# Paged decode in a hybrid decoder step on Trainium2: the order of weighing chunks, the last page gather, the score maxima and the latent division

## The chip, the cores and the metric

The kernel runs on one core of one Trainium2 chip. The metric is the device time of one execution in microseconds (us), as the median of several runs. A profile comes from one further execution that a hardware profiler records.

## The reference

One decoder layer is computed for two groups of requests that share the weights: a prompt of 512 tokens with 16 meta tokens ahead of it, and 8 decode samples of one token, each with a paged past of 4096 positions. The layer has a combined input projection, multi-head latent attention, a retention branch, a gated merge, two layer norms and a convolutional FFN. What the change touches is the latent attention of the 8 samples:

```python
def mla_sample(q_nope, q_rope, c_new, kr_new, c_past, kr_past, w_uk, w_uv):
    ...
    q_abs = jnp.einsum('bthn,chn->bthc', q_nope, w_uk)
    s_past = jnp.einsum('bthc,bsc->bhts', q_abs, c_past) + jnp.einsum('bthr,bsr->bhts', q_rope, kr_past)
    s_new = jnp.einsum('bthc,buc->bhtu', q_abs, c_new) + jnp.einsum('bthr,bur->bhtu', q_rope, kr_new)
    ...
    s = jnp.concatenate([s_past.astype(jnp.float32), s_new], -1) * scale
    p = jax.nn.softmax(s, axis=-1).astype(c_new.dtype)
    o_lat = jnp.einsum('bhts,bsc->bthc', p[..., :past], c_past) + jnp.einsum('bhtu,buc->bthc', p[..., past:], c_new)
```

`c_past` and `kr_past` are the cached latent rows (256 wide) and rotary rows (32 wide) of 32 pages of 128 positions, found by `page_table`.

## The kernel before, in words

The program is written engine by engine; each engine's list is in the order of its code, and semaphores are the only ties. The prompt's projections, retention and attention come first, then the eight samples, then merge, norms and FFN. The change is in the sample stage alone.

**Pages.** GpSimd (POOL) gathers a sample's pages by indirect DMA: four gathers of latent rows (`chunk_pair`, line 656; chunks 0-1, 2-3, 4-5 and 6-7 of 8) and one of rotary rows (`rope_page`, line 663), in the order 0-1, 2-3, rope, 4-5, 6-7. There are three sets of latent page buffers, so a gather for sample b waits until the same pair of chunks of sample b-3 has been weighed (`pv_chunk`) and until all earlier chunks have been turned (`page_turned`). POOL runs these in order: what waits holds all gathers behind it.

**Vector engine (DVE).** `sample_dve(b)` (line 1668) transposes ("turns") the chunks of sample b+1 (`turn_chunk`, L1546) and its rotary rows (`turn_rope`, L1638), and handles the softmax maxima of sample b: `scores_back` (L1644, L1646) takes the maxima over positions, `max_rows` (L1651, L1653) reduces them over partitions after TensorE has transposed them. It also divides the weighted latent of sample b-1 by its sum (`latent_out`, L1663) and inverts the sum of sample b (`inv_sum`, L1659). Eight chunks go through one set of turned tiles in two halves.

**TensorE (PE).** `sample(b)` (line 2590) scores sample b against its turned pages in two halves (`score_half`, L2525: 32 matmuls on latent rows and 4 on rotary rows, each recorded twice), transposes the partial scores (`turn_parts`, L2535), scores the new token (`score_new`, L2542, L2544), transposes the maxima (`max_turn`, L2552) and spreads them (`max_spread`, L2556). Of sample b-1 it sums the exponentials (`sum_spread`, L2561) and weighs the eight chunks (`weigh_chunk`, L2582, and L2587 for the new token). Of sample b-2 it turns the weighted latent (`latent_turn`, L2569).

**ScalarE (ACT).** After `max_spread` it copies the maxima (L1000) and takes the exponentials (L1004), and it copies partial scores (L1012) and weighted latents (L1018) out of PSUM.

The order around the change on PE, for samples 1 to 6, is: first matmul row of the first score half, `max_spread` of the sample before, rest of the first half, `latent_turn`, `sum_spread`, chunks 0 and 1, parts, chunk 2, second half, chunk 3, parts, new token, chunks 4 and 5, `max_turn`, chunks 6 and 7. In the last sample all chunks from 2 on come ahead of the second half.

Of the kernel before, what the change touches and what calls it, by code (L numbers as in the profile page):

```python
# [46 lines left out]
NCH = 8  # L47
# [113 lines left out]
def build(nc, ins, outs):  # L161
    ctx = ExitStack()
    with ctx:
# [211 lines left out]
        S = sems  # L375
# [272 lines left out]
        @block.gpsimd  # L648
        def _(pool):
            chain = Count(S["pool_own_order"])  # L650
            turned = Count(S["ln_turned"])
            
            pair_rows = ins["cache_kv_latent"][0].rearrange("n (q r) c -> (n q) (r c)", q=16)
            rope_rows = ins["cache_k_rope"][0].rearrange("n (q r) c -> (n q) (r c)", q=4)

            def chunk_pair(b, c):

                nc.gpsimd.indirect_dma_start(  # L658
                    out=page_pair(b, c).rearrange("p r c -> p (r c)"), out_offset=None,
                    in_=pair_rows, in_offset=bass.IndirectOffsetOnAxis(ap=IDX2[:, b, c // 2:c // 2 + 1], axis=0)  # L660
                ).then_inc(page_sem(b, c), 16)

            def rope_page(b):
                nc.gpsimd.indirect_dma_start(
                    out=PGR[:, b % 2, :, :].rearrange("p r c -> p (r c)"), out_offset=None, in_=rope_rows,
                    in_offset=bass.IndirectOffsetOnAxis(ap=IDX[:, b, NCH:NCH + 1], axis=0)
                ).then_inc(S[f"rope_pages{b % 2}"], 16)

            pool.wait_ge(S["idx_ready"], 1)
            pool.wait_ge(S["uk_T_ready"], 4)  # L670
            for c in range(0, NCH, 2):
                if c:
                    pool.wait_ge(S["probs_ready"], 6 * NT + c)
                chunk_pair(0, c)
            attn_done = Count(S["attn_done"], start=1)
            pool.wait_ge(attn_done.sem, attn_done.after(4))
            pool.wait_ge(S["out_stored"], 16 * 7)
            rope_page(0)
            for b in range(1, DEC):
                for c in range(0, NCH, 2):  # L680
                    if b >= 3:
                        pool.wait_ge(S["pv_chunk"], (b - 3) * NCH + c + 2)
                    pool.sem_inc(S["go_on"])
                    turned = (b - 1) * NCH + c
                    if turned > 0:
                        pool.wait_ge(S["page_turned"], turned)
                    chunk_pair(b, c)
                    if c == 2:
                        if b >= 2:
                            pool.wait_ge(S["rope_turned"], b - 1)  # L690
                        rope_page(b)
# [554 lines left out]
        def _(dve):  # L1246
# [6 lines left out]
            def lo(n, nk=8):  # L1253

                at_, ks = place(n, nk)
                dve.wait_ge(whi.sem, whi.after())
                V.tensor_tensor(WL[:, at_, ks], RAW[:, at_, ks], WH[:, at_, ks].bitcast(F32), ALU.subtract  # L1257
                                ).then_inc(s_wsplit, 1)
# [381 lines left out]
            def scores_back(par, b):  # L1640

                dve.wait_ge(s_full.sem, s_full.after())
                new = PS[0:DEC, 6, 256:264]
                V.tensor_scalar(new, new, SMALL[0:DEC, b + 16:b + 17], None, ALU.add).then_inc(S["s_bank_free"], 1)  # L1644
                dve.wait_ge(bank_free.sem, bank_free.after())
                V.reduce_max(SSM[:, par, 0:8], PS[:, 6, 0:264].rearrange("p (k h) -> p h k", h=HEADS), AX  # L1646
                             ).then_inc(S["mx_ready"], 1)

            def max_rows(par):
                dve.wait_ge(mxt.sem, mxt.after())  # L1650
                V.reduce_max(SSM[0:8, par, 8:9], PS[0:8, 7, 0:P], AX).then_inc(chain.sem, 1)  # L1651
                dve.wait_ge(chain.sem, chain.after())
                V.tensor_scalar(SSM[0:8, par, 16:24], IDENT[0:8, 0:8], SSM[0:8, par, 8:9], None, ALU.mult  # L1653
                                ).then_inc(S["dg_ready"], 1)
# [13 lines left out]
            def sample_dve(b):  # L1668

                par, more = b % 2, b + 1 < DEC  # L1670
                if more:
                    for c in range(4):
                        turn_chunk(b + 1, c)
                scores_back(par, b)
                if more:
                    turn_rope(b + 1)
                max_rows(par)
                if more:
                    turn_chunk(b + 1, 4)
                    turn_chunk(b + 1, 5)  # L1680
                else:
                    dve.wait_ge(S["ab_hi"], 1)
                    V.tensor_tensor(BL[:], BT[:, :, DEAD:], BH[:].bitcast(F32), ALU.subtract).then_inc(S["ab_split"], 1)
                    lo(N_MERGE + 1, 4)
                if more:
                    turn_chunk(b + 1, 6)
                    turn_chunk(b + 1, 7)
                if b:
                    latent_out(1 - par, b - 1)
                inv_sum(par)  # L1690

            attn_done = Count(S["attn_done"], start=1)
# [389 lines left out]
        def _(pe):  # L2082
# [464 lines left out]
            def max_turn(par):  # L2547

                if mx.n:
                    pe.wait_ge(rs.sem, rs.after())  # L2550
                pe.wait_ge(mx.sem, mx.after())
                T.transpose(PS[0:8, 7, 0:P], SSM[:, par, 0:8], IDENT).then_inc(S["mx_turned"], 1)  # L2552
# [37 lines left out]
            def sample(b):  # L2590

                par, prev, last = b % 2, b > 0, b == DEC - 1
                pe.wait_ge(q_staged.sem, q_staged.after())
                score_half(b, 0, range(1))
                if prev:
                    max_spread(1 - par)
                score_half(b, 0, range(1, 9))
                if b >= 2:  # L2600
                    latent_turn(b - 2)
                if prev:
                    sum_spread(1 - par)
                    weigh_chunk(b - 1, 0)
                    weigh_chunk(b - 1, 1)
                turn_parts(0)
                if prev:
                    for c in range(2, NCH if last else 3):
                        weigh_chunk(b - 1, c)
                score_half(b, 1)  # L2610
                if prev and not last:
                    weigh_chunk(b - 1, 3)
                turn_parts(1)
                score_new(b)
                if prev and not last:
                    for c in range(4, NCH):
                        if c == 6:
                            max_turn(par)
                        weigh_chunk(b - 1, c)
                elif not last:  # L2620
                    max_turn(par)

            q_staged, parts = Count(S["q_staged"]), Count(S["parts_back"])
            pe.wait_ge(S["rows_set"], 1)
# [317 lines left out]
```

## Time and profile before

| | us |
|---|---|
| median of 3 runs | 1009.57 (1007.57 to 1011.45) |
| the profiled execution, own time | 1018.73 |
| its span in the trace | 1016.8 |
| from the first score half of sample 0 (403.5) to the last one of sample 7 (509.9) | 106.4 |

Over the span PE is busy for 96%, DVE for 66%, ACT for 39%. A timeline row gives start, duration, engine, line, operation and tiles, number of instructions, and, in brackets, the idle time of the engine just ahead with what ended it. PE's ends are modelled, its starts are recorded. Times are us from the span's start.

### The profile page before, as it was taken

The numbers are of one execution on the slowest core, as the hardware profiler recorded it, in microseconds if no ns is written. First come the engines' busy times: TensorE is split into PE (matmuls) and PEld (weight loads), VectorE is DVE, ScalarE is ACT, GpSimd is POOL, SyncE is SP. The second block draws the span as 40 slices with busy tenths as digits, with TensorE's granted clock in tenths as the row PEclk, the third lists the DMA queues.
The fourth block names the chain that finished last, engine by engine and source line by source line (L and its number), as shares of the span: only waits on it lengthen the run. The fifth ranks groups of instructions, "written<-read, shape, count | busy, mean of one in ns | idle before, by whom it ended". The sixth has DMA issues, their size and how long they took to land.

```text
span 1016.8 us, 22255 instructions
## 1 busy us (share of the span) xinstructions
PE 971.4 (96%) x9135; PEld 896.2 (88%) x9135; DVE 672.7 (66%) x1070; ACT 396.1 (39%) x881; POOL 39.1 (4%) x44
## 2 busy tenths in 40 slices
PE   5999999989999997799999999999999999999996
PEld 5999999977989896456579999999999999999995
DVE  7747754875556556888746668697773335767567
ACT  4522433425152434233332413566651124565331
POOL 0000000000000011333100000000000000000000
PEclk9999999999999998899999999999999999999998
DMA  9541466041405145999463744214333332332643
GB/s 259 171 118 33 105 150 154 17 110 37 122 26 152 42 145 186 365 359 355 170 211 105 252 122 127 76 51 124 83 94 93 91 100 79 105 102 58 191 114 132
DMA packets 174918, 136.89 MB, mean 135 GB/s; under 512 B 18723, under 2 KB 162952, under 8 KB 170472
## 3 DMA queue, kind: packets, MB, share of 16 engines
q1 hardware_dynamic: 166586, 93.47, 33.1%
q0 software_dynamic: 5760, 37.75, 9.9%
q10 hardware_dynamic: 2502, 4.68, 1.3%
q8 instruction: 51, 0.84, 0.3%
q14 instruction: 19, 0.16, 0.0%
HBM read 124.18 MB, written 11.80 MB: 134 GB/s over the span
## 4 chain that ended last, share of the span: by engine, by line
PE 79%; DVE 12%; issue 5%; ACT 2%; DMA 1%; DVEq 0%; another core or an unknown queue 0%; POOL 0%; SPq 0%; ACTq 0%; POOLq 0%
PE PS L2094 33%; PE PS L2807 8%; PE PS L2347 7%; PE PS L2869 6%; PE PS L2582 3%; PE PS L2525 3%; PE PS L2702 2%; DVE w_lo L1257 2%; PE PS L2105 2%; PE PS L2392 1%; PE PS L2142 1%; PE PS L2231 1%; PE PS L2451 1%; PE PS L2373 1%; PE PS L2384 1%
## 5 line engine op out<-in xcount | busy, mean ns | idle before, releaser
L1257 DVE TENSOR_TENSOR w_lo<-w_raw,w_hi 128x2048 fp32r<-128x2048 f32 (+3 forms) x65 | 125.9, 1937 | 59.4 <-ACT w_hi L708 47.9
L2094 PE MATMUL PS<-x_hi,w_hi 128*128 128x262 f32 (+1 forms) x704 | 152.3, 290 | 0.7 <-DVE w_lo L1257 0.7
L708 ACT ACTIVATE w_hi<-w_raw 128x2048 fp32r<-128x2048 f32 (+3 forms) x59 | 94.6, 1603 | 147.3 <-PE PS L2094 88.3
L2094 PE MATMUL PS<-x_lo,w_hi 128*128 128x262 f32 (+1 forms) x704 | 148.7, 285 | 0.0
L2094 PE MATMUL PS<-x_hi,w_lo 128*128 128x262 f32 (+1 forms) x704 | 148.4, 284 | 0.0
L2094 PEld LDWEIGHTS PS<-x_hi,w_hi 128*128 128x128 f32 x704 | 112.4, 189 | 3.7 <-issue 1.6
L2094 PEld LDWEIGHTS PS<-x_lo,w_hi 128*128 128x128 f32 x704 | 112.0, 189 | 0.0
L2094 PEld LDWEIGHTS PS<-x_hi,w_lo 128*128 128x128 f32 x704 | 111.8, 189 | 0.0
L2347 PE MATMUL PS<-x_hi,w_hi 128*128 128x262 f32 (+1 forms) x256 | 78.6, 307 | 0.0
L2347 PE MATMUL PS<-x_hi,w_lo 128*128 128x262 f32 (+1 forms) x256 | 73.4, 287 | 0.0
L2347 PE MATMUL PS<-x_lo,w_hi 128*128 128x262 f32 (+1 forms) x256 | 73.3, 286 | 0.0
L1546 DVE STREAM_TRANSPOSE pages_T<-pages_c 128x1024 f32<-128x1024 f32 x48 | 55.2, 1203 | 1.9 <-PE PS L2347 1.8
L2525 PE MATMUL PS<-pages_T,q_blocks 128*32 128x128 f32 x1024 | 42.5, 292 | 8.6 <-ACT q_blocks L994 5.5
L2347 PEld LDWEIGHTS PS<-x_hi,w_hi 128*128 128x128 f32 x256 | 48.9, 191 | 0.6
L2347 PEld LDWEIGHTS PS<-x_lo,w_hi 128*128 128x128 f32 x256 | 49.0, 191 | 0.1
L2347 PEld LDWEIGHTS PS<-x_hi,w_lo 128*128 128x128 f32 x256 | 49.0, 191 | 0.0
L2525 PEld LDWEIGHTS PS<-pages_T,q_blocks 128*32 128x32 f32 x1024 | 32.0, 116 | 18.4 <-issue 16.0
L2869 PE MATMUL PS<-ffn_hi,w_hi 128*128 128x268 f32 (+1 forms) x160 | 45.9, 287 | 0.0
L2869 PE MATMUL PS<-ffn_hi,w_lo 128*128 128x268 f32 (+1 forms) x160 | 45.5, 284 | 0.0
L2869 PE MATMUL PS<-ffn_lo,w_hi 128*128 128x268 f32 (+1 forms) x160 | 45.4, 284 | 0.0
L658 POOL DMA_INDIRECT pages_c<-in_cache_kv_latent_dram,page_pair_rows x24 | 23.9, 996 | 414.1 <-DVE w_uk_T L1593 363.0
L1867 DVE SCALAR_TENSOR_TENSOR conv_acc<-a_rows,conv_T,conv_acc 128x516 f32<-128x516 f32 x22 | 16.5, 752 | 34.5 <-ACT conv_acc L1123 34.5
(389 smaller groups left out, 2369.8 us busy)
## 6 DMA issues: line engine op xcount, KB each, us to landing
w_raw<-in_w_ffn_in_dram SPq DMA_DIRECT2D x44, 512.0 KB, 4.6
w_raw<-in_w_in_dram SPq DMA_DIRECT2D x37, 512.0 KB, 6.9
w_raw<-in_w_ffn_out_dram SPq DMA_DIRECT2D x28, 320.0 KB, 3.7
w_raw<-in_w_o_dram SPq DMA_DIRECT2D x12, 512.0 KB, 4.9
w_raw<-in_w_ffn_out_dram SPq DMA_DIRECT2D x16, 384.0 KB, 3.9
gate_scratch<-gate_out ACTq DMA_DIRECT2D x8, 524.0 KB, 3.0
gates<-gate_scratch SPq DMA_DIRECT2D x8, 524.0 KB, 8.8
x_T_scratch<-x_sum_T SPq DMA_DIRECT2D x1, 2144.0 KB, 7.5
```

The lines of the kernel that those rows point to most:

```text
L658: nc.gpsimd.indirect_dma_start(out=page_pair(b, c).rearrange("p r c -> p (r c)"), out_offset=None, in_=pair_rows, in_offset=bass.IndirectO ...
L708: nc.scalar.activation(WH[:, at_, ks], RAW[:, at_, ks], ACT.Copy).then_inc(s_whi, 1)
L1257: V.tensor_tensor(WL[:, at_, ks], RAW[:, at_, ks], WH[:, at_, ks].bitcast(F32), ALU.subtract).then_inc(s_wsplit, 1)
L1546: V.transpose(CT[:, :, :, c, :].rearrange("p r k i -> p (r k) i"), page(b, c).rearrange("p r (k j) -> p (r k) j", j=32)).then_inc(S["page_ ...
L2094: last = T.matmul(PS[:, bank, 0:n], w[:, par, kw + k, m * P:(m + 1) * P], x[:, k0 + k, half * n:(half + 1) * n], start=start and k == 0 an ...
L2105: last = T.matmul(PS[:, 2 * p + half, 0:HALF], a, b[:, half * HALF:(half + 1) * HALF], start=i == 0, stop=i == len(lhs) - 1)
L2347: last = T.matmul(PS[:, half, 0:n], w[:, par, k, m * P:(m + 1) * P], x[:, k, c0:c0 + n], start=k == 0 and w is WH and j == 0, stop=k == 7 ...
L2525: last = T.matmul(PS[32 * r:32 * r + 32, 4 + a, 0:P], QBD[:, par, k, :], pages.rearrange("p c i -> p (c i)"), start=k == 0, stop=k == 8, s ...
L2582: last = T.matmul(PS[g:g + 32, pv_bank(b), :], PB[:, par, k:k + 4, :].rearrange("p k h -> p (k h)"), page(b, c)[:, r:r + 2, :].rearrange(" ...
L2702: last = T.matmul(PS[:, O_BANK[j % 4], 0:c.stop - c.start], w[:, buf(n), k, m * P:(m + 1) * P], x[:, k, c], start=k == 0 and w is WH and i ...
L2807: last = T.matmul(PS[:, bank, 0:LHALF], w[:, k, :], x[:, k], start=start and k == 0 and i == 0 and w is hi_, stop=k == 3 and w is lo_, ski ...
L2869: last = T.matmul(PS[:, q % 4, 0:c.stop - c.start], w[:, buf(N_F2O + j), k, m * P:(m + 1) * P], x[:, s * hk + k, c], start=s == 0 and k == ...
```

## The change

Four pieces of order and one new wait, all in the sample stage:

- PE, `sample`: chunk 3 of the sample before is weighed ahead of the second score half and no longer behind it; the chunks behind move up by one, so that chunk 4 follows the second half and only chunk 7 stands behind `max_turn`. `max_spread` stands ahead of the whole first half.
- POOL: from sample 3 on, the gather of chunks 6-7 of sample b also waits until the first score half of sample b-1 is done.
- DVE: `max_rows` stands ahead of `turn_rope`, and `latent_out` stands between the turns of chunks 5 and 6 and no longer behind chunk 7.

```diff
                 for c in range(0, NCH, 2):
                     if b >= 3:
                         pool.wait_ge(S["pv_chunk"], (b - 3) * NCH + c + 2)
+                        if c == NCH - 2:
+                            pool.wait_ge(S["half_scored"], 2 * b - 1)
                     pool.sem_inc(S["go_on"])
...
                 scores_back(par, b)
+                max_rows(par)
                 if more:
                     turn_rope(b + 1)
-                max_rows(par)
-                if more:
                     turn_chunk(b + 1, 4)
                     turn_chunk(b + 1, 5)
                 else:
                     dve.wait_ge(S["ab_hi"], 1)
                     V.tensor_tensor(BL[:], BT[:, :, DEAD:], BH[:].bitcast(F32), ALU.subtract).then_inc(S["ab_split"], 1)
                     lo(N_MERGE + 1, 4)
+                if b:
+                    latent_out(1 - par, b - 1)
                 if more:
                     turn_chunk(b + 1, 6)
                     turn_chunk(b + 1, 7)
-                if b:
-                    latent_out(1 - par, b - 1)
                 inv_sum(par)
...
                 pe.wait_ge(q_staged.sem, q_staged.after())
-                score_half(b, 0, range(1))
                 if prev:
                     max_spread(1 - par)
-                score_half(b, 0, range(1, 9))
+                score_half(b, 0)
                 if b >= 2:
                     latent_turn(b - 2)
                 if prev:
...
                 turn_parts(0)
                 if prev:
-                    for c in range(2, NCH if last else 3):
+                    for c in range(2, NCH if last else 4):
                         weigh_chunk(b - 1, c)
                 score_half(b, 1)
                 if prev and not last:
-                    weigh_chunk(b - 1, 3)
+                    weigh_chunk(b - 1, 4)
                 turn_parts(1)
                 score_new(b)
                 if prev and not last:
-                    for c in range(4, NCH):
-                        if c == 6:
-                            max_turn(par)
+                    for c in range(5, NCH - 1):
                         weigh_chunk(b - 1, c)
-                elif not last:
+                if not last:
                     max_turn(par)
+                if prev and not last:
+                    weigh_chunk(b - 1, NCH - 1)
```

The lines of the changed kernel are numbered one or two higher than those of the kernel before from the inserted lines on. The order of PE from one `max_turn` (L2552) to the `latent_turn` (L2569) of the next sample, before (a chunk is two L2582):

```order
L2552 MATMUL PS<-square_consts,sm 8x128 [waits mx_ready,rs_ready]
L2582 MATMUL PS<-pages_c,p_sample 32x512 x4
L2587 MATMUL PS<-c_tok_135,p_sample 8x256
L2525 MATMUL PS<-pages_T,q_blocks 32x128 [waits page_turned,q_staged]
L2525 MATMUL PS<-pages_T,q_blocks 32x128 x3
L2556 MATMUL PS<-sm,square_consts 128x8 [waits dg_ready]
L2525 MATMUL PS<-pages_T,q_blocks 32x128 x28
L2525 MATMUL PS<-rope_T,q_blocks 32x128 [waits rope_turned]
L2525 MATMUL PS<-rope_T,q_blocks 32x128 x3
L2569 MATMUL PS<-small_consts,out_parts 128x8 [waits o_parts]
```

and now:

```order
L2553 MATMUL PS<-square_consts,sm 8x128 [waits mx_ready,rs_ready]
L2583 MATMUL PS<-pages_c,p_sample 32x512 x2
L2588 MATMUL PS<-c_tok_135,p_sample 8x256
L2557 MATMUL PS<-sm,square_consts 128x8 [waits dg_ready,q_staged]
L2526 MATMUL PS<-pages_T,q_blocks 32x128 [waits page_turned]
L2526 MATMUL PS<-pages_T,q_blocks 32x128 x31
L2526 MATMUL PS<-rope_T,q_blocks 32x128 [waits rope_turned]
L2526 MATMUL PS<-rope_T,q_blocks 32x128 x3
L2570 MATMUL PS<-small_consts,out_parts 128x8 [waits o_parts]
```

One weighing chunk (two matmuls) has left the stretch behind the turn of the maxima, and the spread of the maxima has moved ahead of the first four score matmuls.

The order of DVE from one score reduction (L1644) to the next, before:

```order
L1644 TENSOR_SCALAR PS<-PS,small_consts 8x8 [waits s_full]
L1646 TENSOR_REDUCE sm<-PS 128x8 [waits s_bank_free]
L1638 STREAM_TRANSPOSE rope_T<-pages_r 128x8x4x32 [waits half_scored,rope_pages1]
L1651 TENSOR_REDUCE sm<-PS 8x1 [waits mx_turned]
L1653 TENSOR_SCALAR sm<-square_consts,sm 8x8 [waits dve_own_order]
L1546 STREAM_TRANSPOSE pages_T<-pages_c 128x32x32 [waits half_scored,pages_landed1_4] x2
L1546 STREAM_TRANSPOSE pages_T<-pages_c 128x32x32 [waits half_scored,pages_landed1_6] x2
L1663 TENSOR_TENSOR o_lat<-PS,sm 128x16 [waits lat_turned]
L1659 RECIPROCAL sm<-PS 128x8 [waits sum_spread]
L1546 STREAM_TRANSPOSE pages_T<-pages_c 128x32x32 [waits half_scored,first_pages_landed1] x2
L1546 STREAM_TRANSPOSE pages_T<-pages_c 128x32x32 [waits half_scored,pages_landed0_2] x2
```

and now:

```order
L1646 TENSOR_SCALAR PS<-PS,small_consts 8x8 [waits s_full]
L1648 TENSOR_REDUCE sm<-PS 128x8 [waits s_bank_free]
L1653 TENSOR_REDUCE sm<-PS 8x1 [waits mx_turned]
L1655 TENSOR_SCALAR sm<-square_consts,sm 8x8 [waits dve_own_order]
L1640 STREAM_TRANSPOSE rope_T<-pages_r 128x8x4x32 [waits half_scored,rope_pages1]
L1548 STREAM_TRANSPOSE pages_T<-pages_c 128x32x32 [waits half_scored,pages_landed1_4] x2
L1665 TENSOR_TENSOR o_lat<-PS,sm 128x16 [waits lat_turned]
L1548 STREAM_TRANSPOSE pages_T<-pages_c 128x32x32 [waits half_scored,pages_landed1_6] x2
L1661 RECIPROCAL sm<-PS 128x8 [waits sum_spread]
L1548 STREAM_TRANSPOSE pages_T<-pages_c 128x32x32 [waits half_scored,first_pages_landed1] x2
L1548 STREAM_TRANSPOSE pages_T<-pages_c 128x32x32 [waits half_scored,pages_landed0_2] x2
```

The rotary turn now stands behind the two small steps on the maxima, and the latent division, which waits for PE's latent turn, now stands ahead of two page turns.

## Rows read from the trace of the kernel before

**Rows 1.** The page's part 1, the whole span.

```profile
span 1016.8 us, 22255 instructions
PE 971.4 (96%) x9135; PEld 896.2 (88%) x9135; DVE 672.7 (66%) x1070; ACT 396.1 (39%) x881; POOL 39.1 (4%) x44
```

**Rows 2.** Busy by stretch: us, PE, PEld, DVE, ACT, POOL; clock; DMA share; GB/s.

```profile
444.80:458.50 13.70, 12.90 (x262) 7.78 (x261) 11.59 (x16) 4.42 (x24) 4.67 (x6) 1.00 0.94 344
```

**Rows 3.** Timeline of PE: the latent turns in samples 2 and 7.

```profile
435.56 1.06 PE L2569 MATMUL PS<-small_consts,out_parts 128*128 128x8 f32 x8
...
502.09 1.06 PE L2569 MATMUL PS<-small_consts,out_parts 128*128 128x8 f32 x8
```

**Rows 4.** Timeline of PE, first score half of sample 3, to its latent turn.

```profile
444.89 0.43 PE L2525 MATMUL PS<-pages_T,q_blocks 128*32 128x128 f32 x8
445.25 0.38 PE L2556 MATMUL PS<-sm,square_consts 8*128 8x8 f32 x2
445.56 1.07 PE L2525 MATMUL PS<-pages_T,q_blocks 128*32 128x128 f32 x29
446.96 0.63 PE L2525 MATMUL PS<-pages_T,q_blocks 128*32 128x128 f32 x12 [0.33 <-issue]
...
449.26 1.06 PE L2569 MATMUL PS<-small_consts,out_parts 128*128 128x8 f32 x8
```

**Rows 5.** Timeline of PE, the same stretch of sample 6.

```profile
486.59 0.43 PE L2525 MATMUL PS<-pages_T,q_blocks 128*32 128x128 f32 x8
...
487.26 1.74 PE L2525 MATMUL PS<-pages_T,q_blocks 128*32 128x128 f32 x56
...
489.15 1.23 PE L2569 MATMUL PS<-small_consts,out_parts 128*128 128x8 f32 x8
```

**Rows 6.** Timeline of ACT: the copy behind the spread maxima, samples 3 and 6.

```profile
446.98 0.18 ACT L1000 ACTIVATE sm<-PS 128x8 f32<-128x8 f32 x1 [1.39 <-PE PS L2556]
...
487.38 0.18 ACT L1000 ACTIVATE sm<-PS 128x8 f32<-128x8 f32 x1
```

**Rows 7.** Timeline of POOL: rotary and last gathers beside sample 3, rotary beside sample 6.

```profile
443.99 0.94 POOL L664 DMA_INDIRECT pages_r<-in_cache_k_rope_dram,page_rows  x1 [0.30 <-issue]
...
447.13 0.94 POOL L658 DMA_INDIRECT pages_c<-in_cache_kv_latent_dram,page_pair_rows  x1 [0.97 <-DVE pages_T L1546]
...
484.39 0.94 POOL L664 DMA_INDIRECT pages_r<-in_cache_k_rope_dram,page_rows  x1 [0.30 <-issue]
```

**Rows 8.** Timeline of DVE, samples 3 and 5.

```profile
450.36 0.19 DVE L1663 TENSOR_TENSOR o_lat<-PS,sm 128x16 f32<-128x16 f32 x1 [1.24 <-PE PS L2569]
450.58 0.21 DVE L1659 RECIPROCAL sm<-PS 128x8 f32<-128x8 f32 x1
450.70 4.58 DVE L1546 STREAM_TRANSPOSE pages_T<-pages_c 128x1024 f32<-128x1024 f32 x4
456.05 0.22 DVE L1644 TENSOR_SCALAR PS<-PS,small_consts 8x8 f32<-8x8 f32 x1 [0.76 <-PE PS L2544]
...
485.18 0.28 DVE L1651 TENSOR_REDUCE sm<-PS 8x1 f32<-8x128 f32 x1 [0.60 <-PE PS L2552]
485.50 0.22 DVE L1653 TENSOR_SCALAR sm<-square_consts,sm 8x8 f32<-8x8 f32 x1
```

**Rows 9.** Timeline of PE: turned maxima of sample 3 to sample 4's scores; of sample 5.

```profile
456.88 0.27 PE L2552 MATMUL PS<-square_consts,sm 128*8 128x128 f32 x1
457.08 1.06 PE L2582 MATMUL PS<-pages_c_slot,p_sample 128*32 128x512 f32 x8
458.08 0.59 PE L2587 MATMUL PS<-c_tok,p_sample 8*8 8x256 f32 x2
458.60 0.43 PE L2525 MATMUL PS<-pages_T,q_blocks 128*32 128x128 f32 x8
...
484.87 0.27 PE L2552 MATMUL PS<-square_consts,sm 128*8 128x128 f32 x1
```

**Rows 10.** Timeline of PE: the spread maxima in sample 1.

```profile
418.12 0.59 PE L2556 MATMUL PS<-sm,square_consts 8*128 8x8 f32 x2 [0.63 <-DVE sm L1653]
```

## The prediction

> **What bounds the kernel now.** The page's first part shows PE busy for 96% of the span [rows 1], so a change of order gains only where PE stands still or runs slowly, or where the engine that feeds it is late. The change touches the samples alone, so I went on to their timelines. In sample 3's cycle PE is busy 12.90 of 13.70 us, DVE 11.59, and the DMA engines 94% [rows 2]: three resources are near their limit, at the full granted clock (1.00, the 2.4 GHz level). From the latent turn of sample 2 (435.56) to that of sample 7 (502.09) are 66.53 us for five cycles [rows 3], 13.3 each.
>
> What the reader should see next is that PE's busy time is partly slow time. The first score half of sample 3 runs from 444.89 to its latent turn at 449.26, 4.37 us [rows 4]; the same work in sample 6 takes 486.59 to 489.15, 2.56 us [rows 5]. So 1.81 us are lost in sample 3. PE stops at 446.63, after 29 score records, and goes on at 446.96 with nothing named as the cause [rows 4]; ACT, which waits for the spread maxima, starts at 446.98 although their matmul was recorded at 445.25 [rows 6, 4]. In sample 6 ACT starts at 487.38. Both starts are 2.99 us after a rotary gather began on POOL (443.99 and 484.39 [rows 7]). A pause tied to the gathers is my reading; that PE's matmul does not signal until then is an inference from two equal distances, not something that the rows show. The last gather starts at 447.13, inside the slow half [rows 7].
>
> A cycle without pauses, from latent turn to latent turn, is 449.26 to 458.60 [rows 4, 9], 9.34, plus the quick half of 2.56: **11.90 us**. Five of them are 59.5, so 66.53 holds about 7.0 us of pauses.
>
> **The change, part by part.**
>
> *Chunk 3 ahead of the second half; one chunk behind the maxima.* No matmul is added. Between the turn of the maxima and the next first half stood 0.20 + 1.00 (two chunks) + 0.52 = 1.72 us [rows 9]; with one chunk it is 1.22. The half microsecond moves to the stretch ahead of the second half. The maxima must be spread by then: DVE's two steps end at 485.72 when the turn started at 484.87 [rows 8, 9], 0.85 later, less than 1.22. So the spread, now ahead of the whole half, does not wait, and ACT's exponentials start about 0.36 us earlier in the half (445.25 less 444.89 [rows 4]). In sample 2 this first shows: 0.5 gained.
>
> *Maxima ahead of the rotary turn.* In sample 1, where PE waited 0.63 us for DVE [rows 10], the wait should mostly go: I take 0.4 of it, since PE now waits at the spread itself and not after four score matmuls. Elsewhere DVE stands idle for the turn instead (0.60 in sample 5 [rows 8]) and the rotary turn follows. It is still ready long before the last four matmuls of the half.
>
> *The last gather.* It now waits for the first half of the sample before, and so starts behind it. Queued behind it on POOL are the gathers 0-1 of the next sample, which anyway wait for chunk 1, weighed after that half. Chunks 2-3, the rotary rows and 4-5 are freed earlier, because chunks 3 and 5 are weighed earlier. Nothing starts in the first half any more. The new wait's price is small: the turn that needs the pages comes a cycle later.
>
> *The latent division ahead of two turns.* This is the part with a cost. `latent_out` waits for PE's latent turn, which stands behind the first half. Behind it on DVE are now two page turns, the reciprocal, four page turns, the score maxima; and PE's turn of the maxima waits for these. That closes a **loop**. From the start of the latent turn: to the division 450.36 - 449.26 = 1.10 [rows 8, 4]; division 0.22; two turns, half of 4.58, 2.29; reciprocal 0.12; four turns 4.55; so the score step stands at 8.28. From it to the turn of the maxima 456.88 - 456.05 = 0.83 [rows 8, 9]. Then 1.22 and the quick half of 2.56: **12.89 us**. Before, the two turns lay outside the loop, which then took 11.1 with 1.72 and the quick half. PE also meets a wait ahead of the second half (the last turn ends at 3.6 us, PE is there at 2.9), but it is hidden: by the old distances PE would come to the maxima at 8.9, DVE at 9.11.
>
> *The sum.* If the pauses leave the path, five cycles of 12.89 are 64.45, against 66.53: 2.1 gained. Sample 2's first half lies ahead of these cycles; its 1.8 and the 0.5 go too, and 0.4 in sample 1. Together 4.8. Against that stands the pause itself, which I don't expect to vanish: the rotary gather, 8.43 us after the latent turn before (443.99 less 435.56 [rows 7, 3]), follows chunk 3, which no longer waits for a half of some 2.3 (2.56 without the spread); so it starts near 6.1, and 2.99 later is 9.1, just where PE signals the turned maxima. Its cost there lies between nothing and a whole pause of 1.8; the nearest row is sample 6, where the distance of 2.99 fell upon ACT's natural start and cost nothing, so I take 0.4 per cycle, 2.0 in five. That leaves 2.8 us. The sum is against the profiled execution (1018.73, span 1016.8), which is 9.16 us above the median; taken over to the median it gives 1009.57 - 2.8 = **1006.8 us**.
>
> **The rivals.**
>
> *The pauses stay in the first half.* For this speaks that in sample 3 PE stops at 446.63, ahead of the last gather's start at 447.13 [rows 4, 7], so the last gather can't be the cause of the first stop. Against it speaks that the earlier gathers move as well. Then each first half keeps 4.37, and the loop is 14.70: five are 73.5, 7.0 more than now, less 0.9 in samples 1 and 2: **1015.7, slower**. It decides if a first half after sample 2 still takes over about 3.2 us. The Trainium skill, "SBUF — State Buffer", section "Who interferes with whom", holds that DMA never contends with a compute engine and that PE waits on no one. By that rule no move of a gather can quicken a score half, and this rival would be the outcome. The trace does not settle it, as its row says "issue".
>
> *The timed runs hardly pause.* The profiled execution is 9.16 us longer than the median; the seven pauses in five cycles and the 1.8 ahead of them are 8.8. If recording makes them, the timed cycle is 11.90 already, and the new loop costs 0.99 x 5 less 0.9, 4.1: **1013.6**, DVE being the bound. Against it: the excess may lie anywhere in the span.
>
> *The transfers become the bound.* The DMA engines are busy 0.94 x 13.70 = 12.9 us per cycle [rows 2], as long as the new loop. With the last gather held back, they may idle a microsecond per cycle; then the cycle is about 13.9 and five cost 3.0 more than now: 1009.57 + 3.0 - 2.7 = **about 1010**, and late pages could make it 1013. Against it: a gather is turned some ten microseconds after it starts. By the Trainium skill, "DMA: Bandwidth & Descriptors", section "Anatomy of one DMA — SWDGE (gpsimd) path", data move at 436 GB/s; for the 344 GB/s x 13.70 us moved here that would be an estimated 10.8 us per cycle, and this rival would fall.
>
> *The loop does not bind.* If the latent turn comes early enough for DVE not to wait, PE's 11.90 is left: 7.0 + 1.8 + 0.9 gained, **999.9**. The order of DVE speaks against it.
>
> **How the numbers follow.** Forecast (1004.8 to 1009) 0.42; pauses stay 0.17; pauses mostly absent in timed runs 0.25; transfers 0.07; no loop 0.09. About 0.5%, 5.05 us, is what a measurement of this kernel can tell from no change. Faster by more: the last case, and a sixth of the forecast: 0.16. Slower by more: three quarters of the first rival, a quarter of the second, part of the third: 0.22. The rest, 0.62, is the same. The range runs from 1002.5, below the forecast without any pause, to 1014.5, which takes in the second rival and half of the first.
>
> **What would show it.** Right: first halves of about 2.6 us in samples 2 to 5; DVE idle ahead of the latent division for the latent turn, then two page turns, and hardly idle ahead of the score step; a wait of under 1 us on PE ahead of the second half; cycles near 13. The POOL gather of chunks 6-7 starts after PE's rotary score matmuls. Wrong: first halves still above 4 us (first rival), cycles under 12.5 (no loop), or DVE waiting for pages (third).

## The result, and the profile after

The changed kernel takes 1014.71 us (median of 4 runs, 1011.69 to 1015.47), beside 1009.36 for the kernel before (4 runs): ratio 1.0043, 95% interval 1.0028 to 1.0058. That is **slower**, by 0.43%. The interval leaves out no change, and no run of one kernel lies among those of the other; but the difference is under the 0.5% that the prediction took as the least it could tell. The ratios here and below are formed from the single runs and are not the quotients of two medians (1.0053 here). Forecast were 1006.8 and a range up to 1014.5; the time lies just above it. The recorded execution took 1011.69, the lowest of the four, so its profile shows the changed kernel at the fast end of its runs. Beside the last three experiments one run of the kernel before took 1881.26 us, a slow run that no ratio uses.

The page's first part, of the changed kernel, answers to [rows 1]; PE's busy time fell and the span with it, but that is against an execution of the kernel before that turns out to be unusual (below).

```profile
span 1009.9 us, 22255 instructions
PE 963.2 (95%) x9135; PEld 891.3 (88%) x9135; DVE 671.8 (67%) x1070; ACT 395.2 (39%) x881; POOL 39.1 (4%) x44
```

Busy time of one cycle without a pause, from latent turn to latent turn (columns as in [rows 2]):

```profile
441.45:454.41 12.96, 12.00 (x265) 7.35 (x261) 11.46 (x16) 4.25 (x27) 4.68 (x5) 1.00 0.98 380
```

The first score halves are quick now: the cycle is 12.96 us, and PE stands idle for 0.96 of it. Where, its timeline shows (start, duration, then as in [rows 4]); it answers to [rows 4, 9] and has the latent turns of [rows 3] as its first and last lines:

```profile
428.49 1.06 PE L2570 MATMUL PS<-small_consts,out_parts 128*128 128x8 f32 x8
...
437.33 0.27 PE L2553 MATMUL PS<-square_consts,sm 128*8 128x128 f32 x1 [0.96 <-DVE sm L1648]
437.53 1.05 PE L2583 MATMUL PS<-pages_c,p_sample 128*32 128x512 f32 x4
438.51 0.59 PE L2588 MATMUL PS<-c_tok,p_sample 8*8 8x256 f32 x2
439.04 0.38 PE L2557 MATMUL PS<-sm,square_consts 8*128 8x8 f32 x2
439.35 1.95 PE L2526 MATMUL PS<-pages_T,q_blocks 128*32 128x128 f32 x64
441.12 0.40 PE L2526 MATMUL PS<-rope_T,q_blocks 128*32 128x128 f32 x8
441.45 1.06 PE L2570 MATMUL PS<-small_consts,out_parts 128*128 128x8 f32 x8
...
474.60 0.20 PE L2545 MATMUL PS<-q_blocks,rope_new_T 128*8 128x8 f32 x2
476.99 1.06 PE L2583 MATMUL PS<-pages_c,p_sample 128*32 128x512 f32 x8 [2.19 <-issue]
...
495.08 1.06 PE L2570 MATMUL PS<-small_consts,out_parts 128*128 128x8 f32 x8
```

From 428.49 to 495.08 are 66.59 us for five cycles: four of 12.96 and one of 14.74, which holds the pause of 2.19. DVE, in the same recording, answers to [rows 8]:

```profile
442.55 0.18 DVE L1665 TENSOR_TENSOR o_lat<-PS,sm 128x16 f32<-128x16 f32 x1 [0.98 <-PE PS L2570]
442.64 2.36 DVE L1548 STREAM_TRANSPOSE pages_T<-pages_c 128x1024 f32<-128x1024 f32 x2
444.92 0.17 DVE L1661 RECIPROCAL sm<-PS 128x8 f32<-128x8 f32 x1
445.02 4.56 DVE L1548 STREAM_TRANSPOSE pages_T<-pages_c 128x1024 f32<-128x1024 f32 x4
449.50 0.18 DVE L1646 TENSOR_SCALAR PS<-PS,small_consts 8x8 f32<-8x8 f32 x1
449.71 0.43 DVE L1648 TENSOR_REDUCE sm<-PS 128x8 f32<-128x264 f32 x1
```

The division waits for the latent turn, and the score step at 449.50 waits for nothing but DVE itself: the loop is closed, PE waits in it, and 12.96 stands where 12.89 was worked out.

### The profile page after: what moved, and what is told of

It is laid out like the page before. It is cut to its first block, busy times and chain, and to the rows that moved or that the text cites. A ratio compares the mean times of both kernels' runs of the same rounds, so it can differ in the third digit from the quotient of the medians.

```text
span 1009.9 us, 22255 instructions
## 1 busy us (share of the span) xinstructions
PE 963.2 (95%) x9135; PEld 891.3 (88%) x9135; DVE 671.8 (67%) x1070; ACT 395.2 (39%) x881; POOL 39.1 (4%) x44
## 4 chain that ended last, share of the span: by engine, by line
PE 75%; DVE 16%; issue 6%; ACT 1%; DMA 1%; DVEq 0%; POOL 0%; SPq 0%; ACTq 0%; POOLq 0%
PE PS L2095 33%; PE PS L2807 8%; PE PS L2348 7%; PE PS L2869 6%; DVE pages_T L1548 3%; DVE w_lo L1259 2%; PE PS L2702 2%; PE PS L2583 2%; PE PS L2526 2%; PE PS L2106 2%; PE PS L2393 1%; PE PS L2232 1%; PE PS L2452 1%; PE PS L2385 1%; PE PS L2374 1%
## 5 line engine op out<-in xcount | busy, mean ns | idle before, releaser
L2526 PE MATMUL PS<-pages_T,q_blocks 128*32 128x128 f32 x1024 | 34.4, 290 | 6.3 <-ACT q_blocks L996 5.8
```

The lines of the kernel that those rows point to most:

```text
L2526: last = T.matmul(PS[32 * r:32 * r + 32, 4 + a, 0:P], QBD[:, par, k, :], pages.rearrange("p c i -> p (c i)"), start=k == 0, stop=k == 8, s ...
```

## The experiments

All ratios are to the kernel before, run on the same chip beside them, with 95% intervals. Not all groups of experiments ran on the same chip, so kernels of different groups are compared by their ratios.

**The kernel before once more.** No edit.

> The kernel before, unchanged, with a fresh profile. Theory A (the pauses of TensorE differ from execution to execution, and the first profile of before had unusually many): the fresh profile has fewer of them, the five cycles from the latent turn of sample 2 to that of sample 7 take 60 to 64 us and no longer 66.5, and its own time is 1007 to 1012 us. Theory B (every recorded execution has them, the timed ones not): five cycles of 66 to 67 again and an own time near 1018, with a median near 1009.5.

Median 1010.50 (ratio 1.0006, 0.9995 to 1.0017), and the fresh recording took 1009.91. Its latent turns:

```profile
430.07 1.06 PE L2569 MATMUL PS<-small_consts,out_parts 128*128 128x8 f32 x8
...
493.35 1.06 PE L2569 MATMUL PS<-small_consts,out_parts 128*128 128x8 f32 x8
```

Five cycles take 63.28 us and not 66.53 [rows 3]; none of its first halves is slow as that of [rows 4]. So theory A: the execution that the prediction was read from was unusual. None of the 107 executions of the kernel before beside all experiments but the last three took over 1012.67, against its 1018.73. But pauses are there, at other places: cycles of 11.61, 13.79, 12.16, 13.06 and 12.67.

**The division back, and the division alone.** The first takes the changed kernel; the second is the opposite move in the kernel before. The edit of the first:

```diff
-                if b:
-                    latent_out(1 - par, b - 1)
                 if more:
                     turn_chunk(b + 1, 6)
                     turn_chunk(b + 1, 7)
+                if b:
+                    latent_out(1 - par, b - 1)
```

> The changed kernel with the latent division back behind the turn of chunk 7. Loop theory (DVE's loop through the division makes the cycle of 12.96 us): PE no longer waits 0.96 us for the score maxima, the cycle falls to about 12 us, five cycles give back 4 to 5 us, median 1007 to 1010. Rival (the held gather or the transfers set the cycle, the loop only fills it): the cycle stays near 13 and the median near 1014.

> The kernel before with nothing but the latent division moved between the turns of chunks 5 and 6. Loop theory: 8.28 + 0.83 + 1.72 (two chunks behind the maxima) + 2.56 = 13.4 us per cycle, 1.5 more than the 11.90 without pauses; five of them up to 7 us, and less by what pauses the runs of before hold anyway: 1013 to 1017, so at least all of the change's loss from this edit alone. Rival (the loss lies in another part): 1009 to 1010, as before.

The division alone: 1013.47, ratio 1.0035 (1.0021 to 1.0050), five cycles of 13.11 to 13.22, 65.70 together. PE waits for the maxima by 0.96 in cycle after cycle:

```profile
440.11 0.27 PE L2552 MATMUL PS<-square_consts,sm 128*8 128x128 f32 x1 [0.96 <-DVE sm L1646]
453.23 0.27 PE L2552 MATMUL PS<-square_consts,sm 128*8 128x128 f32 x1 [0.96 <-DVE sm L1646]
466.35 0.27 PE L2552 MATMUL PS<-square_consts,sm 128*8 128x128 f32 x1 [0.96 <-DVE sm L1646]
```

That is the loop as expected, 0.3 shorter than worked out. With the division put back, the loop is gone, yet the time is 1012.75, ratio 1.0037 (1.0022 to 1.0052): a miss for the loop theory alone. The recorded cycles are 11.88, 12.50, 13.20, 15.82 and 11.64; PE pauses again where it no longer waits. Something other than DVE was next in line.

**What the pauses are.** The page lists, for the whole changed kernel, a DMA queue of instructions (packets, MB, share):

```profile
q8 instruction: 51, 0.84, 0.3%
```

That is 16 KB a packet. In the 4.0 us ahead of the pause at 474.6 the queue list shows no such packet; in 474.6 to 475.7 it shows

```profile
q0 software_dynamic: 49, 0.39, 97.3%
q8 instruction: 1, 0.02, 5.4%
```

and 1.3 us after the end of that stretch PE goes on (476.99). Through the other recordings the pauses follow the same pattern, but for the slow halves of the first one: from sample 1 on each whose row says "issue", nothing else having ended it, ends 1.15 to 1.61 us after such a packet has ended, and they stand 127 or 128 matmul records apart, or a multiple. **Theory F** followed: TensorE's program arrives in blocks of 16 KB; a block's packet stands in the DMA queues with the gathers, and when it is late, PE stops at the end of the block before. Two tests: take transfer time away, and move the block ends.

**Half the gather bytes** in the kernel before, the changed one, and the changed one with the division back. What is left out stands in the first expectation.

```diff
+            half_rows = ins["cache_kv_latent"][0].rearrange("n (q r) c -> (n q) (r c)", q=32)
...
+                out, rows = page_pair(b, c).rearrange("p r c -> p (r c)"), pair_rows
+                if b >= 3:
+                    out, rows = out[:, 0:4 * KVL], half_rows
...
```

> The kernel before, with gathers of latent pages that carry half the bytes from sample 3 on (half of each page row is left out, so the numbers of samples 3 to 7 are others). Theory F (PE's pauses are late 16 KB blocks of its own program, whose packets stand behind gather packets in the DMA queues): the pauses of 0.4 us and more at these places go, cycles fall to 11.6 to 11.8 us, five cycles to 58 to 59.5 instead of 63.3, median 1004 to 1006. Rival (the pauses have nothing to do with the gathers): the same pauses, median 1009 to 1011.

> The changed kernel with the same halved gathers from sample 3 on. Theory F with the loop through the latent division: the pause of 2.2 us in sample 5 goes, but the cycle stays at 12.9 to 13.0, five cycles near 64.8, median 1010.5 to 1013. Rival (transfers set the cycle of 12.96): cycles below 12.5, median below 1009.

> The changed kernel with the latent division behind the turn of chunk 7 and halved gathers from sample 3 on. Theory F: neither loop nor late blocks, cycles 11.6 to 11.9 us, five near 59, median 1004 to 1007, as the kernel before with halved gathers. Rival (something else in the new order costs what the division's return did not give back): 1009 or more.

1005.40 (ratio 0.9950, 0.9931 to 0.9969), 1012.73 (1.0026, 1.0015 to 1.0037) and 1006.24 (0.9964, 0.9952 to 0.9977). Theory F's forecast holds in all three: with the DMA engines 69% busy the kernel before has four cycles of 11.61 or 11.62 and one of 12.24, the third kernel four of 11.88 or 11.89 and one of 12.40, with a pause of 0.55; both lost over 4 us. The changed kernel keeps 12.96 in four of five cycles, so its loop is not a matter of transfers. The windows of one cycle, first of the kernel before with half the bytes, then of the third kernel:

```profile
441.97:453.58 11.61, 11.61 (x265) 7.12 (x261) 11.37 (x16) 4.35 (x26) 4.69 (x6) 1.00 0.69 231
```

```profile
441.25:453.13 11.88, 11.65 (x265) 7.52 (x261) 11.36 (x16) 4.25 (x27) 4.68 (x5) 1.00 0.69 224
```

The 0.27 between them is the new order's own cost, at a place that the prediction priced wrong. In the first of the two, a pair of chunks stands behind the turned maxima:

```profile
437.70 0.27 PE L2556 MATMUL PS<-square_consts,sm 128*8 128x128 f32 x1
437.90 1.06 PE L2586 MATMUL PS<-pages_c,p_sample 128*32 128x512 f32 x8
438.89 0.59 PE L2591 MATMUL PS<-c_tok,p_sample 8*8 8x256 f32 x2
439.42 0.43 PE L2529 MATMUL PS<-pages_T,q_blocks 128*32 128x128 f32 x8
```

Two chunks (eight records) take 438.89 - 437.90 = 0.99 us; in the changed kernel above, one chunk (four records) takes 438.51 - 437.53 = 0.98. The two of a pair write different rows of PSUM and run side by side, so one chunk less shortens nothing: 1.71 us from the maxima to what follows, and 1.72 before. Ahead of the maxima the moved chunk does cost: from the latent turn to the turn of the maxima it is 7.76 us in the third kernel (441.25 to 449.01) and 7.34 in the kernel before (441.97 to 449.31), and 0.23 of that is a wait for DVE's maxima:

```profile
449.01 0.27 PE L2557 MATMUL PS<-square_consts,sm 128*8 128x128 f32 x1 [0.23 <-DVE sm L1652]
```

The spread ahead of the half gives 0.14 back (2.41 from there to the next latent turn, against 2.55), which leaves 0.42 - 0.01 - 0.14 = 0.27.

**Parts of the change.** Order and maxima (the changed kernel without the held gather and with the division back); the order alone; the held gather alone; the changed kernel without the held gather. The edits are those pieces of the diff.

> The kernel before with TensorE's new order and the maxima ahead of the rotary turn, without the held gather and with the latent division where it was. Theory F: these edits give PE nothing by themselves; the held gather bunches the transfers, and without it the blocks come as in the kernel before: 1008 to 1011. Rival (the new order on PE is itself what makes the late blocks worse): 1012 to 1014, as with the held gather.

> The kernel before with nothing but TensorE's new order. Theory: the two weighings of a pair of chunks run side by side, so that one chunk behind the turn of the maxima takes as long as two did, 0.98 us; the cycle without pauses is 11.88 and not 11.61, 0.27 more in six cycles: 1.5 us, 1011 to 1012. Rival (the order saves the half microsecond behind the maxima, as predicted): 1007 to 1009.

> The kernel before with nothing but the held last gather. Theory F: the gather starts later and stands nearer to the next three, so that blocks wait longer in the queues; cost 1 to 2.5 us, as between the pairs of kernels that differ by it (1014.7 and 1012.0; 1012.8 and 1011.6): 1011 to 1012.5. Rival (the wait costs nothing by itself): 1009.5 to 1010.5.

> The changed kernel without the new wait of the last gather. Loop theory: the cycle stays at 12.9 to 13.0, median 1013 to 1015, and the wait is worth nothing. Rival 1 (the wait takes transfer time away): 1009 to 1011. Rival 2 (the wait keeps pauses out of the first score half, as the prediction supposed): first halves of 4 us come back and the median is 1016 or more.

| kernel | median, us | ratio (95%) |
|---|---|---|
| order and maxima | 1011.57 | 1.0015 (1.0004 to 1.0027) |
| order alone | 1013.19 | 1.0024 (1.0012 to 1.0035) |
| held gather alone | 1011.07 | 0.9998 (0.9981 to 1.0014) |
| division alone (above) | 1013.47 | 1.0035 (1.0021 to 1.0050) |
| all but the held gather | 1011.95 | 1.0026 (1.0009 to 1.0042) |
| all but the division (above) | 1012.75 | 1.0037 (1.0022 to 1.0052) |
| all | 1014.71 | 1.0043 (1.0028 to 1.0058) |

The order costs, 2.4 us by its ratio; the 1.5 us that its 0.27 per cycle would give lie within the interval. With the maxima ahead it may cost less, but the intervals overlap; its 1011.57 lies between the two expectations. The division costs. The held gather alone costs nothing that can be told: its median of 1011.07 would fit the expectation of a cost, its ratio fits the rival's none. In the changed kernel it may cost something (1.0043 against 1.0026), but the intervals overlap; that stays open. Without it the cycle in the loop stays (12.96 and 12.97 in three of five), as expected, though the median of 1011.95 is lower than that; and no first half is slow: from first score matmul to latent turn it takes 2.10 us (441.71 to 443.81), as in the changed kernel (439.35 to 441.45).

The pieces don't add up to the whole. PE's wait in the loop and its late blocks can fill the same time: with half the bytes, where few blocks are late, putting the division back gives 6.5 us (1012.73 less 1006.24), with all of them nothing that can be told (ratios 1.0043 and 1.0037).

**The block ends moved.** Unused matmuls, where PE waits ahead of sample 0, shift all that follows in TensorE's program; they write to where the turn of the maxima writes later.

```diff
+            for _ in range(16):
+                T.matmul(PS[0:32, 7, 0:P], IDENT[:, 0:32], QAB[:].rearrange("p a b h -> p (a b h)")[:, 0:P], start=True,
+                         stop=True, skip_group_check=True)
             pe.wait_ge(S["rows_set"], 1)
```

> As with half a block, but 16 unused matmuls, a quarter block. Theory F: all pauses 32 matmul records earlier than in the kernel before, time 1006 to 1013. Rival: places and time as in the kernel before, 1009 to 1011.

> The kernel before, with 32 unused matmuls (128 instructions of TensorE's program, half a 16 KB block) put where TensorE waits ahead of sample 0. Theory F (pauses sit where a 16 KB block of TensorE's program ends): the places of all pauses move 64 matmul records earlier in the program; the pause ahead of L2544 in sample 6 and that ahead of the weighing behind the new token's scores in sample 5 go, others appear in the middle of the second half or of the weighing ahead of it. Time by theory F anything from 1006 to 1013, as each place meets the gathers at another moment. Rival (pauses belong to these instructions): the pauses stay ahead of L2544 and of the weighing, and the time stays 1009 to 1011.

> The kernel before with 48 unused matmuls ahead of sample 0, three quarters of a block. Theory F: the pauses stand 96 matmul records earlier than in the kernel before, about 155 records behind the turn of the maxima in sample 6 (in the second score half) or 28 (in the first); the time is that of the place: 1007 to 1016. Rival (a quarter block was slow for its unused matmuls, not for the place): time grows with their number, above 1016.

A quarter block alone makes the kernel before **slower** by 0.5%: 1015.93, ratio 1.0050 (1.0034 to 1.0065), as much as the whole change does and above the 1006 to 1013 expected. Its timeline of PE shows a pause in each of five samples, inside the transposes of the partial scores, six records earlier each time (244, 238, 232, 226 and 220 records behind the turn of the maxima):

```profile
441.24 0.22 PE L2535 MATMUL PS<-square_consts,score_parts 128*32 128x32 f32 x2 [1.30 <-issue]
454.28 0.28 PE L2535 MATMUL PS<-square_consts,score_parts 128*32 128x32 f32 x9 [1.31 <-issue]
467.64 0.30 PE L2535 MATMUL PS<-square_consts,score_parts 128*32 128x32 f32 x12 [1.61 <-issue]
481.07 0.35 PE L2535 MATMUL PS<-square_consts,score_parts 128*32 128x32 f32 x19 [1.31 <-issue]
493.92 0.41 PE L2535 MATMUL PS<-square_consts,score_parts 128*32 128x32 f32 x26 [0.86 <-issue]
```

Between two of them PE runs 255 records, two blocks:

```profile
454.28:467.64 13.36, 11.75 (x255) 7.24 (x256) 11.37 (x15) 4.36 (x24) 4.93 (x6) 1.00 0.96 365
```

The pause of sample 6 stands 220 records behind the turn of the maxima; in the unshifted kernel 251, so 31 earlier for 32 records put in. Half a block gives 188, and 1010.65 (1.0005, 0.9992 to 1.0019); three quarters 156, and 1010.77 (1.0002, 0.9993 to 1.0012). So the cost does not grow with the number of matmuls, and the pauses move with the place of the block ends.

Not all of the quarter block's cost is pauses, though. Its recorded execution is 7.10 us longer than the fresh one of the kernel before (1017.01 less 1009.91). The five cycles hold 2.69 of that (65.97 from 433.62 to 499.59, against 63.28); 3.55 lie ahead of them, as the latent turn of sample 2 stands at 433.62 and not at 430.07. There, behind the start of sample 0, only one pause of 0.18 shows, and the mean granted clock was lower (0.80 from 399.07 on, against 0.84 from 398.76). Whether the block ends or the unused matmuls themselves caused that part is not shown.

**The changed kernel with moved block ends.** The same edit there.

> The changed kernel with 16 unused matmuls ahead of sample 0. Theory F with the loop: the pauses move to the transposes behind the second score half, where TensorE waits 0.96 us for DVE anyway; what is above that delays the maxima, so cycles of 13 to 14: 1013 to 1017. The difference to the kernel before at the same phase (1015.9) is then within 0.3%, and not +0.43%. Rival (the change costs 4 to 5 us at any phase): 1019 to 1021.

> The changed kernel with 32 unused matmuls ahead of sample 0, half a block. Theory F with the loop: cycles stay near 12.96 (the loop) where a pause is under the wait of 0.96, longer only in one or two samples: 1012 to 1015, so 2 to 4 us above the kernel before at the same phase (1010.65). Rival: as the changed kernel or worse, 1015 to 1017.

At a quarter block the changed kernel takes 1015.99 (1.0061, 1.0048 to 1.0075); the kernel before at that place had 1.0050 (1.0034 to 1.0065): no difference that can be told. At half a block it takes 1013.50 (1.0033, 1.0021 to 1.0045), where the kernel before had 1.0005 (0.9992 to 1.0019), and here no pause shows; all five cycles are 12.96 or 12.97, which is the bare loop:

```profile
443.49:456.46 12.97, 11.89 (x266) 7.27 (x262) 11.47 (x16) 4.26 (x27) 4.69 (x5) 1.00 0.99 377
```

**A try at a better one.** In the recording with three quarters of a block five cycles took only 60.59, but the unused matmuls ran 4 us into sample 0. By turns on two groups of PSUM rows they run side by side:

```diff
...
+                T.matmul(PS[32 * (k % 2):32 * (k % 2) + 32, 7, 0:P], IDENT[:, 0:32],
...
```

> The kernel before at three quarters of a block, with the 48 unused matmuls written by turns to two groups of PSUM rows, so that two run side by side. In s48 they lasted from 398.1 to 408.4, 4 us past the moment at which sample 0 could start, and its first turn of the maxima came at 416.28 and not at 414.02. Theory: they now end near 403.5, sample 0 starts as before and the 2.3 us are not paid: 1008 to 1009, below both kernels. Rival (its quicker cycles were chance of one recording): 1010 to 1011.

> The same with 40 unused matmuls, 0.625 of a block, between the phases of s32 and s48. By theory F the pauses stand about 172 records behind the turn of the maxima in sample 6, in the second score half as in both neighbours: 1008 to 1010. Rival: as the kernel before, 1010 to 1011.

> The same with 56 unused matmuls, 0.875 of a block. By theory F the pauses stand about 140 records behind the turn of the maxima in sample 6, at the start of the second half: 1008 to 1011. Rival: as the kernel before, 1010 to 1011.

1009.44 (0.9997, 0.9983 to 1.0011), 1012.39 (1.0029, 1.0016 to 1.0042) and 1011.64 (1.0019, 1.0006 to 1.0032). None beats the kernel before, and all three lie above what theory F led to expect: it gave the places of the pauses, not the time. Neighbouring places differ by 0.3%, and a single recording with short cycles is no median.

## Why the prediction was wrong

**The step that failed** is "66.53 holds about 7.0 us of pauses", carried over to the median together with the 1.8 of sample 2. The recorded execution held lost time that the timed ones mostly did not: five cycles take 63.28 in the fresh recording, whose 1009.91 lies near the median. The latent turn of sample 2 stands at 435.56 [rows 3] and at 430.07 there, that of sample 7 at 502.09 and at 493.35. So 5.49 us of the excess lie ahead of the five cycles and 3.25 in them, together 8.74 of the 8.82 by which the two executions differ (1018.73, 1009.91). The new loop, at 64.8 for five, takes 1.5 more than 63.28 and not 2.1 less than 66.53. Without the 3.25 and sample 2's 1.8 the forecast gain of 2.8 is a loss of 2.25: the sign turned on this step. The recording's own time, 9.2 us above the median, was the warning; the text put the chance that it matters at 0.25 and took the rest.

The signs named for a right forecast could not show this. First halves of 2.41, DVE idle ahead of the division and not ahead of the score step, cycles of 12.96 and a last gather behind the rotary score matmuls (442.35, behind 441.12) all came true; only the wait ahead of the second half is absent. They test the changed kernel, and the step that failed was in the base it was compared with. The five cycles themselves came out as summed, 66.59 for 64.45 and 2.0 of remaining pauses, in part by luck: the 2.0 stood for pauses behind the rotary gathers, and what is there is one late block.

**The loop** was right: 12.89 forecast, 12.96 found. That the sum came this close is luck, as three terms were off and nearly cancelled: the turned maxima to the next half take 1.71 and not 1.22 (the pair of chunks, above), the way to the score step 8.05 and not 8.28, the quick half with its spread 2.41 and not 2.56. PE's cycle without pauses was put at 11.90 and is 11.61.

**The held gather** was priced right, at nothing by itself. What it was to cure, slow first halves, is absent without it too. The distance of 2.99 us behind a rotary gather marks none of the pauses found since; those stand at block ends. What the slow halves of the first recording were stays open: they stand at no block end, and no later recording has such a first half at the full granted clock.

**The maxima ahead of the rotary turn**: in sample 1 the way from the turned maxima to their spread fell from 1.56 us (414.02 to 415.58 in the fresh recording of the kernel before, where the spread waits for DVE as in [rows 10]) to 0.99 (412.52 to 413.51). That is 0.6 for the 0.4 forecast, but it brought nothing here: from the turned maxima to the sum of the exponentials are 4.90 us in both recordings (414.02 to 418.92, 412.52 to 417.42). The granted clock fell to 0.50 in both, 2.49 us behind the turn of the maxima in the first (416.51) and 1.75 in the second (414.27); what the move is worth at the full clock is not shown.

**The rivals.** Two came within about 1 us of 1014.71: "The pauses stay in the first half", 1015.7, and "The timed runs hardly pause", 1013.6. Only the second has the right bound, DVE's loop, and even its reason was wrong in part: recording makes no pauses, since a recording near the median has them too; and the timed runs lose some 4.6 us to them, if half the bytes remove nothing else (1010.03 less 1005.40). "The transfers become the bound" has its share, not by late pages but by late blocks. The estimate of 10.8 us of transfers per cycle that was set against it does not hold here: the DMA engines were busy for 0.98 of the 12.96 us, 12.7, at 380 GB/s. "The loop does not bind" is out. "The pauses stay in the first half" is out: first halves take 2.41 in the changed kernel. The Trainium skill, "SBUF — State Buffer", section "Who interferes with whom", says that DMA never contends with a compute engine and that PE waits on no one. The traces agree for the matmuls themselves: a quick first half of the kernel before takes 2.55 us to its latent turn with all the bytes (427.52 to 430.07) and with half of them (439.42 to 441.97). The pauses at block ends lie outside that rule.

The parts add up for the recordings, not for the medians. The recorded changed kernel reaches the latent turn of sample 2 1.58 us sooner than the fresh recording of the kernel before (428.49, 430.07) and takes 3.31 longer for the five cycles, together the 1.8 by which the two executions differ (1011.69, 1009.91). The medians differ by 4 to 5, and no recording of the changed kernel lies at its median. Where the rest is lost stays open: executions differ by several us, as the ranges show.

## What to carry to other kernels

Hold the profiled execution against the timed ones before any of its idle time enters a sum; where it is far off, record again or read only differences that a second recording shares. A wait moved ahead of work on a second engine can close a loop: add its terms up once round, and compare with the cycle that is there. And where an unrolled loop runs close to full DMA queues, compare two orders at more than one place of the program's blocks, since a shift alone, by a few unused matmuls, moved the time here by as much as the change.

## What the runs showed of the hardware

TensorE's program competes with data. A block of 16 KB, 255 matmul records for two of them, lasts PE some 5.7 us (a cycle of 11.6 us has 261 records); with the DMA engines 94 to 99% busy it came up to 2.2 us late, and with 69% the longest such pause from sample 3 on was 0.55 us. The Trainium skill, "Runtime: NRT & Kernel Launch", section "Instruction fetch mechanics", has the blocks of 16 KiB, which the packets bear out, and calls the cost of crossing from one to the next mostly hidden; here it was not.

A long pause may cost twice. In the recording of order and maxima PE stood still for 2.00 us ahead of 475.46; 1.2 us later its granted clock fell to 0.50, the 1.2 GHz level, for the 6.73 us shown, and the score half in it took 3.8 us, 479.99 to 483.75, where 2.1 is usual:

```profile
473.50:476.60 3.10, 1.14 (x9) 0.24 (x8) 0.89 (x3) 0.00 (x0) 0.54 (x1) 1.00 1.00 388
476.67:483.40 6.73, 6.73 (x73) 3.94 (x76) 6.15 (x7) 2.96 (x18) 1.87 (x2) 0.50 0.92 338
483.40:487.00 3.60, 3.60 (x73) 2.27 (x66) 2.12 (x4) 1.20 (x5) 0.00 (x0) 0.99 0.69 275
```

That the pause caused the fall is not shown: the changed kernel's pause of 2.19 was followed by none (granted clock 1.00 from 467.38 to 482.12). In the changed kernel with half the bytes one half ran at 0.55, mostly at that level, with no late block ahead of it, PE having been busy for 2.44 of the 3.40 us before; that makes the one cycle of 14.63 there:

```profile
452.00:455.40 3.40, 2.44 (x15) 0.60 (x9) 2.88 (x7) 0.17 (x1) 1.84 (x2) 1.00 0.84 254
455.40:459.20 3.80, 3.80 (x73) 3.46 (x73) 2.26 (x3) 2.76 (x18) 0.00 (x0) 0.55 0.51 194
```
